# Attention on one core: GpSimd multiplies a differential head's inverse sum by lambda and applies both factors, and two inversions on VectorE move into the next loop

## What is computed

```python
def diff_attend(q, k, v, lam):
    def blk(qi):
        s = jnp.einsum('bqhmd,bshmd->bhmqs', qi, k).astype(jnp.float32) * (DIFF_HD ** -0.5)
        p = jax.nn.softmax(s, axis=-1)
        a = (p[:, :, 0] - lam * p[:, :, 1]).astype(v.dtype)
        return jnp.einsum('bhqs,bshe->bqhe', a, v)
```

## Time and profile before

| what | value |
|---|---|
| median of 3 runs | 2581.59 us (2568.35 to 2581.72) |
| profiled execution | 2580.6 us, span 2578.9 us, mean granted clock 0.934 |
| attention stages, about | 150 us each |
| 449 to 599 us: TensorE, VectorE, ScalarE, GpSimd busy | 130.4, 97.3, 82.7, 82.5 us |

### The profile page before, as it was taken

How to read it: one execution, slowest core, us unless ns; L and a number is a source line. 1 busy time by engine, 2 the same in 40 slices (tenths; PEclk the granted TensorE clock), 3 DMA queues, 4 the chain that set the end, 5 groups by cost and what they waited for, 6 DMA issues and landing times. The chain is left out here.

```text
span 2578.9 us, 40912 instructions
## 1 busy us (share of the span) xinstructions
PE 2215.9 (86%) x16631; PEld 1860.0 (72%) x16631; DVE 1362.5 (53%) x1905; ACT 954.8 (37%) x1502; POOL 460.7 (18%) x421
## 2 busy tenths in 40 slices
PE   5997587888899999998993878889599898899992
PEld 4986465557899999998982665577477666787782
DVE  5566555764422222235666566654455665645546
ACT  4333134553421122214331255542344554434433
POOL 0046332661000000000164334620100000000002
PEclk8999798989899999998997999899799999999996
DMA  6331763923222233122215710011666877756653
GB/s 220 100 89 30 178 208 96 343 90 87 60 68 67 73 82 82 47 61 65 87 30 126 207 39 1 1 46 54 236 202 222 290 253 267 260 173 201 218 179 148
DMA packets 370843, 340.68 MB, mean 132 GB/s; under 512 B 90593, under 2 KB 339887, under 8 KB 369647
## 3 DMA queue, kind: packets, MB, share of 16 engines
q1 hardware_dynamic: 354447, 279.26, 35.6%
q10 hardware_dynamic: 11520, 41.95, 5.0%
q0 software_dynamic: 4704, 17.04, 1.7%
HBM read 287.42 MB, written 50.79 MB: 131 GB/s over the span
## 5 line engine op out<-in xcount | busy, mean ns | idle before, releaser
L2850 DVE TENSOR_TENSOR w_lo<-w_raw,w_hi 128x2048 fp32r<-128x2048 f32 (+1 forms) x138 | 306.3, 2229 | 124.5 <-ACT w_hi L2690 124.2
L2690 ACT CAST w_hi<-w_raw 128x2048 fp32r<-128x2048 f32 (+1 forms) x138 | 254.6, 1855 | 8.7 <-PE ps L2622 6.1
L2590 PE MATMUL ps<-w_hi,h_hi 128*128 128x512 f32 (+1 forms) x528 | 205.6, 389 | 32.2 <-DVE w_lo L2850 32.2
L2590 PE MATMUL ps<-w_lo,h_hi 128*128 128x512 f32 (+1 forms) x528 | 199.5, 378 | 0.0
L2590 PE MATMUL ps<-w_hi,h_lo 128*128 128x512 f32 (+1 forms) x528 | 199.2, 377 | 0.0
L3130 PE MATMUL ps<-ffn_h_hi,w_hi_ffn 128*128 128x320 f32 x704 | 161.9, 311 | 5.5 <-DVE ffn_h_lo L379 4.2
L3130 PE MATMUL ps<-ffn_h_lo,w_hi_ffn 128*128 128x320 f32 x704 | 161.6, 311 | 0.0
L3130 PE MATMUL ps<-ffn_h_hi,w_lo_ffn 128*128 128x320 f32 x704 | 161.4, 311 | 0.0
L2590 PEld LDWEIGHTS ps<-w_hi,h_hi 128*128 128x128 f32 x528 | 101.2, 192 | 62.8 <-issue 26.5
L1881 DVE TENSOR_REDUCE tm<-ps 128x1 f32<-128x768 f32 (+1 forms) x140 | 111.1, 816 | 41.8 <-PE ps L1777 26.1
L2696 ACT ACTIVATE tokens_then_blocks<-ps 128x256 f32<-128x256 f32 (+2 forms) x84 | 29.0, 345 | 274.1 <-PE ps L2590 231.0
(11 more groups left out here) (480 smaller groups left out, 5277.0 us busy)
## 6 DMA issues: line engine op xcount, KB each, us to landing
w_raw<-in_moe_w_gu SPq DMA_DIRECT2D x186, 512.0 KB, 4.9
w_raw<-in_moe_w_down SPq DMA_DIRECT2D x41, 1024.0 KB, 5.4
G_decay<-in_ada_w ACTq DMA_DIRECT2D x54, 512.0 KB, 5.0
w_ahead<-in_ffn_w_gu SPq DMA_DIRECT2D x44, 512.0 KB, 5.2
slots_h<-tm SPq DMA_DIRECT2D x14, 1024.0 KB, 11.2
slots_y<-tm SPq DMA_DIRECT2D x13, 1024.0 KB, 11.3
w_ahead<-in_ffn_w_down SPq DMA_DIRECT2D x16, 704.0 KB, 4.7
oA<-in_ada_w ACTq DMA_DIRECT2D x20, 512.0 KB, 5.5
```

What stands on the lines that cost most here:

```text
L2590: mm = pe.matmul(ps[:, bank, 0:2 * columns(u)], x[:, k, tile * P:(tile + 1) * P], gate_up(wt, u, k), start=(k == 0 and n == 0), stop=(k == ...
L2690: act.copy(part(whi, n), raw_piece(n)).then_inc(s["w_hi"], 1)
L2850: dve.tensor_tensor(part(wlo, n), raw_piece(n), part(whi, n).bitcast(F32), ALU.subtract).then_inc(s["w_lo"], 1)
```

## The change

VectorE now only inverts the sum of the second map, into a buffer of its own (`inv2`), one tile at a time and with no wait for itself. GpSimd multiplies the inverse by `nlam` in a new one-column instruction, waits for it, and then multiplies y by two per-row scalars in one instruction, the sum of the first map and that product. The inversions of tiles 4 and 0, which stood at the end of the loop that scores the C unit, now stand in the next loop behind `bring(v, 1)` and `least(v + 1, 0)`. No DMA is added, removed or moved.

```diff
                     def join(u, t):
-                        r = ratio[:, C_BEFORE_U[u] % 2, t:t + 1]
-                        pool.wait_ge(s["ratio_in"], joined_count(u, t))
+                        a, r = (q[:, C_BEFORE_U[u] % 2, t:t + 1] for q in (inv2, ratio))
+                        pool.wait_ge(s["inv2_in"], joined_count(u, t))
                         x, y = prob_slot(u, 0, t), prob_slot(u, 1, t)
-                        gated(pool.tensor_scalar(y, y, r, None, ALU.mult))
+                        gated(pool.tensor_tensor(r, a, nlam, ALU.mult))
+                        gated(pool.tensor_scalar(y, y, rs[:, u % 3, t:t + 1], r, ALU.mult, ALU.mult))
                         pool.tensor_tensor(x, x, y, ALU.add).then_inc(s["joined"], 1)
...
-                    def weight_second(u, tiles):
-
-                        dve.wait_ge(s["p_in"], tile_count(u, 1, tiles[-1]))
-                        a, b = min(tiles), max(tiles) + 1
-                        r = ratio[:, C_BEFORE_U[u] % 2, a:b]
-                        chain(dve.reciprocal(r, rs2[:, u % 3, a:b]))
-                        dve.scalar_tensor_tensor(out=r, in0=rs[:, u % 3, a:b], scalar=nlam, in1=r, op0=ALU.mult, op1=ALU.mult
-                                                 ).then_inc(s["ratio_in"], len(tiles))
+                    def invert_second(u, t):
+
+                        dve.wait_ge(s["p_in"], tile_count(u, 1, t))
+                        dve.reciprocal(inv2[:, C_BEFORE_U[u] % 2, t:t + 1], rs2[:, u % 3, t:t + 1]).then_inc(s["inv2_in"], 1)
...
                         if ahead:
                             least(v + 1, 0)
+                        if now and units[v][0] == "C":
+                            invert_second(v, 4)
+                            invert_second(v, 0)
...
-                            weight_second(v + 1, (1,))
+                            invert_second(v + 1, 1)
...
-                            weight_second(v + 1, (2,))
+                            invert_second(v + 1, 2)
...
-                            weight_second(v + 1, (3,))
+                            invert_second(v + 1, 3)
...
                             least(v + 1, 7)
-                            weight_second(v + 1, (4,))
-                            weight_second(v + 1, (0,))
```

More of the change, by code:

```diff
@@ L1610, in attention @@
             second_ctx = gap[3][:, o:o + 2 * P].rearrange("p (u n) -> p u n", u=2)
-            low, rs, rs2, inv, ratio = (gap[2][:, o + a:o + a + u * n].rearrange("p (u n) -> p u n", u=u)
-                                        for a, u, n in ((0, 4, 2), (8, 3, NT), (23, 3, NT), (38, 2, NT), (48, 2, NT)))
+            low, rs, rs2, inv, inv2, ratio = (gap[2][:, o + a:o + a + u * n].rearrange("p (u n) -> p u n", u=u)
+                                              for a, u, n in ((0, 4, 2), (8, 3, NT), (23, 3, NT), (38, 2, NT), (48, 2, NT), (58, 2, NT)))
             RING, NRING, OB = 4, 3, 7
@@ L1714, in values @@
                 return tm[:, k - 2 if k else 0, c0:c0 + HD]
-            with stage(nc, "scores least p_in ratio_in joined turned copied_act copied_dve pv o_sb o_turned o_out chain zeroed filled root inv gated"
+            with stage(nc, "scores least p_in inv2_in joined turned copied_act copied_dve pv o_sb o_turned o_out chain zeroed filled root inv gated"
                        ) as (block, s):
```

## The result

The changed kernel takes 2543.94 us (median of 4 runs, 2542.46 to 2549.16) against 2578.8 us (4 runs, 2568.35 to 2581.72): a ratio of 0.9857, 95% interval 0.9828 to 0.9887, so 35 us less. The profiled execution took 2544.57 us with a span of 2542.9 us. The forecast was 2562 us with a range of 2548 to 2597.

A forecast was written before the change was run, and what follows sets the result against it. In attention, a chain of score, minimum and exponential set the pace, VectorE made late by GpSimd. Eight units at 2.0 us plus 1.2 us twice gave 18.4 us off 2580.6: 2562 us, range 2548 to 2597.

The forecast's parts named there:

- the clock gives back more: Rival, attention stages: fewer TensorE stalls, so up to five clock falls avoided at 3 to 4 us; 2547 us, chance 0.07.
- the first case: GpSimd's two-scalar product takes 0.98 to about 1.4 us; total 2562 us, own range 2547 to 2568, chance 0.42.
- The step on VectorE: Attention stages: with L1889 off VectorE, copies and minima come earlier; 2.0 us in each of eight units.
- The product: GpSimd's join in attention: multiplying y by two per-row scalars takes 0.98 us, like L2919.
- The rival with the old 2.2 us: GpSimd's product in attention stays about as slow and paces the stage; 2582 us, no change, chance 0.31.
- The lock: VectorE's L1889, with two SBUF operands, stands still until GpSimd's running instruction ends; 218 to 1837 ns, median 966.
- The one-column product: GpSimd's new instruction in each join: 0.18 us, or 0.27 us with its wait for itself.
- the move: Inversions of tiles 4 and 0 put into the next loop: gain hidden behind TensorE's order, counted as nothing.

The follow-up runs named there:

- e7_filled: Kernel before plus useless TensorE transposes at the two idle places of each C unit, all waits kept; 2563.1 us, ratio 0.9929.
- e0_after: The changed kernel itself, measured again beside other follow-up kernels on one chip; 2553.6 us, ratio 0.9892.
- e1_two_ops: Kernel before with only GpSimd's product given a second factor of 1.0; L1889 stays on VectorE; 2548.9 us, ratio 0.9882.
- e5b_delay_3: Changed kernel with a useless VectorE minimum behind the inversion of tile 3 alone; 2554.7 us, ratio 0.9894.
- e2_one_tensor: Kernel before with L1889 made a VectorE instruction with one tensor and two per-row scalars; GpSimd's product unchanged; 2584.9 us, ratio 1.001.
- e5_delay_2_3: Changed kernel with a useless VectorE minimum behind the inversions of tiles 2 and 3; 2587.4 us, ratio 1.0014.
- e4_slow_product: Changed kernel with GpSimd's one-column instruction taking both factors and the old one-operation product behind it; 2591.4 us, ratio 1.0033.

## Why the prediction was wrong, point by point

**What failed is one term, the clock.** The rival "the clock gives back more" said that some falls may not come, priced them at 15 us, and then: "The stalls do not all go, so I add none of it." With 2562 that made 2547 the end of the first case, and 2548 that of the range. In the profiles of the changed kernel all falls were gone, five of five, though the stall at `turn(v,1)` had only shrunk, to 0.27 us. e7_filled puts the falls at 18.3 us in profiled distances: from first join to the end of the stage, both layers, the kernel before takes 274.3 us (599.40 - 463.25 and 1714.46 - 1576.29), e7_filled 256.0. That is 3.7 us a fall, inside the 3 to 4 I had priced; what failed is that the sum took none of it. By medians the clock's share is 19.3 us (the ratio of 0.9929), of the 28.9 us that e0_after gains on the same chip; the even split of the gain is that of the profiles. The mechanism was seen and named; the size that it got in the sum, nothing, and its chance (0.07) were the mistake. I had read the fall at 554 us next to the stalls of the pair before. In its own pair it starts right behind the first of two stalls (granted clock 1.00 from 550 to 554 us, 0.53 from 554 to 558). TensorE's timeline of the kernel before:

```profile
553.78 0.74 PE L1781 MATMUL ps<-kC,qC 96*128 96x512 f32 x3 [1.06 <-ACT second_maps L1964]
...
556.20 1.09 PE L1791 MATMUL ps<-cst,sixth_slot 128*128 128x128 f32 x4 [0.82 <-DVE p_turned L1896]
```

In the profiles the falls grow with the stalls at these two places, the last score and `turn(v,1)`, named in this order with typical lengths. None and 0.27 us: no pair of eight (the changed kernel). 0.30 and 0.42: none (e7_filled). 0.30 and 0.55: one (e1_two_ops). None and 1.5: three (e5b_delay_3). 0.35 and 1.4: five (e2_one_tensor). 1.06 and 1.28: five (before). 1.06 and 1.5: seven (e5_delay_2_3). None and 2.25: eight (e4_slow_product). The length of the stalls does not settle a single pair: in the kernel before, those of C1 and C2 in layer 0 have 1.06 and 1.3 us and the clock held. What decides there no run here tells.

**The step on VectorE held.** Forecast 2.0 us a pair, 1.2 more for each first unit, 18.4 us in all. Between e7_filled, which has the full clock and the old chain, and the changed kernel the profiles give 17.8 us (256.0 less 119.11 and 119.12). By medians e7_filled and e0_after stand 9.6 us apart, with intervals that reach 5 and 11 us to either side, so the medians neither confirm nor contradict it.

**The product held, by a choice that could have gone wrong.** 0.98 us was forecast from L2919's rate and 981 ns came. e4_slow_product shows what the choice carried: with 2.2 us in its place the same change costs 0.3%. The rival with the old 2.2 us came out at 2582 us, 1 us above no change; e4_slow_product measured 9 us above. It had the place wrong. I let GpSimd pace at `turn(v,4)`; in e2_one_tensor and e4_slow_product the long wait is at `turn(v,1)`, 1.38 and 2.25 us, for tile 2. I had the number (a gain of 0.3 there and no more) and did not read it as a stall that pulls the clock down.

The rule that I named beside it, "GPSIMD Engine Reference", section "Elementwise — side-by-side cycle accounting" of the Trainium skill, agrees with the slope of the two-operation form measured here, 0.83 ns or 1.0 cycle an element at its 1.2 GHz. The one-operation form, at 2.5 ns an element, is three times slower than the rule has it, and there the measurement decides.

**The lock was real but not sufficient.** The prediction laid both stalls to L1889 and took GpSimd's speed for a condition. Four kernels make a square: L1889 and the slow product 26.97 us a pair (before), the slow product without the lock 26.48 (e2_one_tensor), L1889 with the fast product 25.19 (e1_two_ops), neither 24.92 (the changed kernel). Each limit hides the other, and with the product fast the lock mostly goes away by itself, since GpSimd is idle when L1889 comes.

**The one-column product and the move held.** 189 ns against 0.18; the move costs and gives nothing in the pair. That it stands in the change's title is no measure of its worth.

## What to carry to other kernels

When a chain of engines is tight, price a stall of TensorE twice: its own length, and what a lower clock does to the matmuls behind it. Here, by the profiles, 2 us of stall in 27 cost as much again in clock, and useless filler transposes alone bought 0.7%. When one instruction waits for another engine's lock, look for what makes the other engine's instruction long before moving the first. And try both forms of an instruction on GpSimd, with and without a second operation.

## What the runs showed that I had not expected

On GpSimd a product by one per-row scalar with no second operation takes 2.20 us for 128x768, and with a second multiplication by a constant of 1.0 it takes 0.905 us; with two per-row scalars 0.98 us. The three have the same operand, read and written in place. On one column, two per-row scalars take 340 ns against 189 ns for a product of two tensors. Why the form with fewer operations is the slower one no run here tells.
